# Attention on VectorE: reciprocals of the softmax's sums four steps later, the second bank's sums copied one step later

## The reference

```python
def attend_block(q_nope, q_pe, q_chunk, k_nope, k_pe, v, k_chunk):
    s = jnp.einsum("bqhd,bkhd->bhqk", q_nope, k_nope) + jnp.einsum("bqhr,bkr->bhqk", q_pe, k_pe)
    s = s.astype(jnp.float32) * SM_SCALE
    mask = k_chunk[None, :] <= q_chunk[:, None]
    s = jnp.where(mask[None, None], s, -1e30)
    w = jax.nn.softmax(s, axis=-1).astype(v.dtype)
    return jnp.einsum("bhqk,bkhd->bqhd", w, v)
```

## Time and profile before

| | us |
|---|---|
| median of three runs | 2449.06 |
| the profiled execution, its own time | 2446.93 |
| its span in the profile | 2445.1 |
| PE busy | 2427.2 (99%) |
| DVE busy | 1806.5 (74%) |
| ACT busy | 1283.4 (52%) |
| POOL busy | 537.9 (22%) |

### The profile page before, as it was taken

How to read it: one execution, slowest core, us unless ns; L and a number is a source line. 1 busy time by engine, 2 the same in 40 slices (tenths; PEclk the granted TensorE clock), 3 DMA queues, 4 the chain that set the end, 5 groups by cost and what they waited for, 6 DMA issues and landing times. The chain is left out here.

```text
span 2445.1 us, 44182 instructions
## 1 busy us (share of the span) xinstructions
PE 2427.2 (99%) x17358; PEld 2340.8 (96%) x17358; DVE 1806.5 (74%) x2893; ACT 1283.4 (52%) x2306; POOL 537.9 (22%) x513
## 2 busy tenths in 40 slices
PE   9999999999999999999999999999999999999998
PEld 9999977899999999999999999778999999999998
DVE  8677767778776677677686777687787766776676
ACT  5566355655554454455535763557455544554454
POOL 0024155200112211220201142552002112211212
PEclk9999999999999999999999999999999999999999
DMA  4232200453447634664731221005435456546655
GB/s 164 71 115 73 53 11 20 88 154 106 96 86 139 129 84 98 133 120 90 221 100 52 61 73 54 11 20 115 133 109 114 88 115 132 109 87 121 132 104 185
DMA packets 109740, 242.48 MB, mean 99 GB/s; under 512 B 15536, under 2 KB 18960, under 8 KB 109408
## 3 DMA queue, kind: packets, MB, share of 16 engines
q0 software_dynamic: 48512, 102.26, 23.3%
q1 hardware_dynamic: 60880, 137.37, 18.0%
q10 hardware_dynamic: 144, 0.04, 0.0%
HBM read 147.39 MB, written 94.29 MB: 99 GB/s over the span
## 5 line engine op out<-in xcount | busy, mean ns | idle before, releaser
L3270 DVE TENSOR_TENSOR wlo<-raw_all,whi 128x512 fp32r<-128x512 f32 (+1 forms) x420 | 270.6, 653 | 181.1 <-ACT whi L2308 178.6
L2308 ACT ACTIVATE whi<-raw_all 128x512 fp32r<-128x512 f32 (+1 forms) x420 | 248.6, 599 | 278.4 <-DVE raw_all L3403 88.0
L3792 POOL DMA_DIRECT2D x_scratch<-stage x224 | 200.0, 943 | 839.1 <-DVE stage L3413 694.0
L2361 ACT ACTIVATE stage<-ps 128x536 f32<-128x536 f32 (+1 forms) x224 | 135.5, 612 | 148.6 <-PE ps L1590 143.6
L3413 DVE TENSOR_TENSOR stage<-stage,ps 128x536 f32<-128x536 f32 (+1 forms) x168 | 118.9, 708 | 84.8 <-PE ps L1590 84.0
L2873 DVE TENSOR_REDUCE mxp<-ps 128x1 f32<-128x80 f32 (+10 forms) x376 | 137.1, 376 | 51.7 <-PE ps L1304 47.7
L1113 PE MATMUL ps<-xgh,whi 128*128 128x358 f32 (+1 forms) x720 | 157.2, 326 | 0.0
L1113 PE MATMUL ps<-xgl,whi 128*128 128x358 f32 (+1 forms) x720 | 156.6, 325 | 0.0
L1113 PE MATMUL ps<-xgh,wlo 128*128 128x358 f32 (+1 forms) x720 | 156.5, 325 | 0.0
L1738 ACT ACTIVATE whi<-raw_all 128x1024 fp32r<-128x1024 f32 (+3 forms) x64 | 58.1, 908 | 174.5 <-PE ps L1113 158.0
L1113 PEld LDWEIGHTS ps<-xgl,whi 128*128 128x128 f32 x720 | 124.0, 189 | 0.0
(11 more groups left out here) (948 smaller groups left out, 7799.7 us busy)
## 6 DMA issues: line engine op xcount, KB each, us to landing
raw_all<-in_wst SPq DMA_DIRECT2D x237, 256.0 KB, 3.4
raw_all<-in_wst SPq DMA_DIRECT2D x74, 512.0 KB, 3.6
x_scratch<-stage POOLq DMA_DIRECT2D x120, 268.0 KB, 6.1
x_scratch<-stage POOLq DMA_DIRECT2D x120, 264.0 KB, 6.0
xall<-x_scratch SPq DMA_DIRECT2D x32, 537.0 KB, 8.6
x_scratch<-xall POOLq DMA_DIRECT2D x24, 537.0 KB, 3.5
raw_all<-in_wst POOLq DMA_DIRECT2D x30, 256.0 KB, 5.5
xall<-in_xT SPq DMA_DIRECT2D x8, 537.0 KB, 8.4
```

The costliest lines, as they stand in the source:

```text
L2308: nc.scalar.activation(dst, src, ACT.Copy).then_inc(S["u_hi"], 1)
L2361: nc.scalar.activation(quarters(stage_of(L, g, i, n)[:, 0:N2]), src, ACT.Copy, scale=-1.0 if row else 1.0).then_inc(S["x_copy"], 1)
L3270: V.tensor_tensor(dst, src, hi.bitcast(F32), ALU.subtract).then_inc(S["u_lo"], 1)
L3792: pool.dma_start(x_scr[2 * i + row, :, a:b], stage_of(L, g, i, n)[:, 0:b - a], accum_op=ALU.add).then_inc(S[done], 16)
```

## The change

Three things. A list SUM_LAG gives the number of steps that the copy of the sums stands behind the last pair of a bank: 4, 5, 4 in place of 4 for all; so the copy of the second bank goes from step 12 to step 13 in all 8 heads of both layers. INVERT_AT goes from 10 to 14. In DVE's program step 13 is all_parts, shift_lo, then the copies of the sums, so both the copy and (in heads 2, 4, 6) the reciprocal now stand behind shift_lo. Nothing is added or removed, and no wait or other engine's program is edited.

```diff
 LAG = 3
 OUT_LAG = LAG + 1
+SUM_LAG = [OUT_LAG, OUT_LAG + 1, OUT_LAG]
 MX_AT = list(range(2, 13))
 MX_END = MX_AT[-1] + 1
...
-INVERT_AT = 10
+INVERT_AT = 14
...
                         for n_bank in range(3):
-                            hb, ib = divmod(h * NP + i - OUT_LAG - BANK_LAST[n_bank], NP)
+                            hb, ib = divmod(h * NP + i - SUM_LAG[n_bank] - BANK_LAST[n_bank], NP)
                             if ib == 0 and hb >= 0:
                                 sums_out(hb, n_bank)
                         if h in (2, 4, 6) and i == INVERT_AT:
```

## The result

The changed kernel takes 2463.32 us, the median of six runs (2462.51 to 2467.56), against 2448.47 us for the kernel before in its six. The ratio is 1.0064 with a 95% interval of 1.0051 to 1.0077: slower by 14.9 us. Forecast were +6.9 us (2456.0) and a range up to 2460.5. The direction was right; the size was not, and the measured time lies 2.8 us above the range.

What follows compares the result with a forecast made beforehand. PE, busy for 99% of the span, was taken to bound the kernel. Ordinary heads -1.1, stops +6.8 and head 4 +1.2 gave +6.9 us on 2449.06, so 2456.0 us, range 2451.6 to 2460.5.

Steps and rivals of the forecast that it cites:

- The waits at the transposition all go: PE's 14 attention waits for all_parts vanish, 5.1 us; the sum took -1.1 us, for the eight ordinary heads.
- The shift comes behind reciprocal and store, and PE stops: POOL's second shift issues 1.44 us later; PE stands 1.7 us at heads 3, 5, 7; six times, +6.8 us.
- The clock: PE's clock behind its stops: the prediction had no term for it, so nothing in the sum.
- Head 4, the shift beside the load: Second shift issues behind SP's 512 KB load; price between 0 and 1.6 us, taken as 0.6, twice: +1.2 us.
- The copy behind shift_lo costs nothing: Second bank's copy on DVE, costed at nothing: PE overwrites that bank only some 10 us away.
- the tightest place: DVE's steps 14 to 18 in head 4: load_q had 0.38 us idle ahead, so comes 0.6 us later.
- the cover that I had named for head 4: PE itself starts that head later; without this, PE waits some 0.2 us for the keys' cast, twice.
- D (slower still): Rival, chance 0.10: shift DMAs wait for load and store writes, 1.6 us in head 4, landings 2.2 elsewhere; +13, 2462.
- The signs that I had named: Transposition waits under 0.5 us; scores of heads 3, 5, 7 wait for POOL's shift DMA, six times 1.5 to 2.3 us.

Runs made afterwards that it cites:

- e7_copy_in_gap: As e3_shifts_first, with the second bank's copy between all_parts and shift_lo for heads 0 to 6; 2441.24 us, ratio 0.9970.
- e4_load_later: The changed kernel, but SP issues the 512 KB load behind the sums of head 4, in step 4 of head 5; 2456.70 us, ratio 1.0036.
- e3_shifts_first: The changed kernel, but POOL issues few_shifts ahead of store_inverse; 2444.60 us, ratio 0.9984.
- e9_copy_in_gap_again: e7_copy_in_gap unchanged, run once more against the kernel before; 2440.06 us, ratio 0.9965.
- e2_recip_only: The kernel before with only the reciprocals moved to step 14, the copy staying in step 12; 2460.82 us, ratio 1.0052.
- e6_load_ahead: As e3_shifts_first, but SP issues the 512 KB load between its own shift DMAs in head 4, both y_fill_lo done in step 6; 2457.90 us, ratio 1.0039.

## Why the prediction went wrong

I use one more reading: the pitch from one transposition to the next, from the weight loads of that line. In layer 0, from head 2 to head 3, the kernel before, the changed kernel, and e7_copy_in_gap:

```profile
356.45 0.14 PEld L1310 LDWEIGHTS ps<-ident,mx 128*128 128x128 f32 x1 [0.87 <-DVE mx L2880]
...
376.08 0.14 PEld L1310 LDWEIGHTS ps<-ident,mx 128*128 128x128 f32 x1 [0.45 <-DVE mx L2880]
```

```profile
354.88 0.14 PEld L1311 LDWEIGHTS ps<-ident,mx 128*128 128x128 f32 x1
...
376.16 0.14 PEld L1311 LDWEIGHTS ps<-ident,mx 128*128 128x128 f32 x1
```

```profile
354.90 0.14 PEld L1311 LDWEIGHTS ps<-ident,mx 128*128 128x128 f32 x1
...
374.13 0.14 PEld L1311 LDWEIGHTS ps<-ident,mx 128*128 128x128 f32 x1
```

The pitch is 19.63 us before, 21.28 with a stop of 1.84, and 19.23 in e7_copy_in_gap, which has neither the wait nor the stop.

- **The waits at the transposition all go.** Right, but the size was too small. I took 5.1 us from PE's row of waits. The pitches of an ordinary head are 19.69 before and 19.20 after: 0.49 us, where the row had 0.19. Over all fourteen, the pitches of e7 are 7.9 us shorter than those before (0.3 to 0.5 each in ordinary heads, 0.7 to 0.8 in those with a reciprocal). The eight ordinary heads alone gain 3.3 us, where the sum had 1.1. The row counts only the time in which no matmul was modelled as running. The row of the weight loads before, for sixteen waits, was nearer:

```profile
PEld ps L1310 <- DVE mx L2880: 9.3, 16, 0.9
```

- **The shift comes behind reciprocal and store, and PE stops.** Right in mechanism, order and place. The second shift was forecast for 1.44 us later than before, that is at 359.64 where the transposition is at 355.85; it was issued at 358.91 with a transposition at 355.01, 0.1 us off. At heads 3 and 7 I forecast a stop of 1.7 us; they were 1.84, 2.31, 1.53 and 1.57, mean 1.81.
- **The clock.** This is the first of the two steps that failed, and the larger: the sum had nothing for it, without a reason, and it cost 5.3 us (three falls). I had treated PE's waiting as the whole price of a stop. The longest wait of PE in the attention before was 0.6 us, so no row could show a fall; but stops of a length that the trace does not hold should have widened the range upwards.
- **Head 4, the shift beside the load.** This is the second. I priced the neighbourhood of the load at 0 to 1.6 us and took 0.6. The second shift's landing took 2.1 us more in layer 0 (3.7 us in place of 1.6) and 2.5 more in layer 1 (4.1), above my upper end. I had taken that end from what a broadcast of 268 KB pays there, and a DMA of 0.2 KB paid more. The stops were 3.69 and 4.13 us where the sum had 2.3 each. That is 3.2 us, and two of the three falls of the clock stand behind these stops. e4_load_later, which takes the load away, comes to 2456.7 us, inside the range.
- **The copy behind shift_lo costs nothing.** Wrong. It pushes all that follows on DVE, the casts of the keys at the start of the next head last, and PE waits in step 2 of head 6 (L1305, 1.0 us in two waits). The view gives no cause for these waits; in layer 0 the cast of the keys ends at 427.8 and PE goes on at 428.0. I had called head 4 the tightest place; at the end of head 5 stand the division of the outputs and four small tasks. By the pitches of the changed kernel and of e7, where the copy stands in the gap, the stretches behind the transpositions of heads 3 and 5, which hold no stop, are longer by 0.41 + 0.69 + 0.31 + 0.64 = 2.0 us. Where the cover that I had named for head 4 is gone (e3_shifts_first, no stall), PE waits 0.3 us there in each layer; I had said 0.2.

Together, against the profile before: -7.9 (transpositions) + 15.1 (stops) + 5.3 (clock) + 2.0 (casts) = +14.5 us, and +14.9 was measured. That it comes so near is partly luck, for the terms come from single executions and the 14.9 from medians. The profiled execution had +16.7: 14.8 of them lie in the attention, by its pitches and the stops of head 7. The rest lies outside, where single executions differ anyway: between the last transposition of layer 0 and the first of layer 1, which is mostly the MLP, lie 1076.35 us before and 1077.64 to 1081.60 us in the kernels without stops in the attention (e7_copy_in_gap 1077.97, its repetition 1081.60). The repetition's 3.6 us more are seen in its trace: PE waits 1.80 us for ACT until 510.9 us, outside the attention, and the clock falls behind it for 3.4 us. The 1.3 us or more that all of them lie above the kernel before I leave unexplained.

Of my rivals, D (slower still) priced the change at 2462, near the measured time, but by luck: it had 1.6 us for the load, too little, landings of 2.2 us at heads 3 and 7, where three of the four took 1.5 to 1.8, and nothing for the clock. The signs that I had named came, all but two: the view names no DMA, and the stops reach 4.1 us and add up to 15.1 where I had 2.3 and 10 to 12.

## What to carry to other kernels

Before an instruction of the vector engine is moved, follow its semaphore to the engine that issues DMAs and look at what is queued there behind it: a store that nobody needs for 10 us held up two DMAs of 0.1 and 0.2 KB that the next head needed in 2, and the cure was one change of order. Keep small, urgent DMAs away from the start of a large one. A stop of PE of some 2 us or more may cost another 1.7 us through the clock, as it did in this kernel, and the row of a short wait can understate its price; the pitch of a repeated stage measures both.

## What the runs showed of the hardware that was not expected

- A DMA of POOL of 0.1 to 0.2 KB, issued from 0.1 us ahead of to 0.5 us behind SP's 512 KB load, landed in 2.8 to 4.2 us in place of 1.5 to 2.3; issued 0.27 and 0.29 us ahead, it landed in 1.6.
- The clock fell to 1.2 GHz for about 3.4 us behind every stop of PE of 2.9 to 4.1 us, behind none of 1.9 us or less at the heads' starts, and in between behind 2.20, 2.23, 2.27 and 2.31 but not behind 2.45 and 2.49 us. Outside the attention it fell behind a stop of 1.80 us in e9_copy_in_gap_again and not behind one of 1.71 in e2_recip_only. In e6_load_ahead it was down for 6.8 us behind two waits of 2.1 and 0.7 us with some 1 us of work between them. The falls began 0.05 to 1.4 us after PE went on. What decides between 1.8 and 2.5 us stays open.
- A subtraction of 128x512 on DVE, 0.68 us in the median, took 3.16 us in e6_load_ahead, once in each layer, where it ran beside POOL's subtraction of 64x1296; it ended 0.3 us after POOL's, which took 3.30 us in place of 2.95. It was not tried by itself.
